# Weight split ring of a two-block model on one core: five slots for four, both engines four pieces ahead for three, six raw slots for five

## The reference

```python
def first_block(x, p, ...):
    for i in range(2):                                   # "layer a"
        h = mixer_block(h, ...)     # rmsnorm, h @ w_in, retention and gated delta rule, w_br_*, w_out
        u = rmsnorm(h, norm_ffn[i])
        h = h + (swiglu(u, ...) if i == 0 else moe(u, ...))   # 8 experts, top 2
        h = h + sigmoid(rmsnorm(h, norm_ple[i]) @ w_ple_gate[i]) * (p[i] @ w_ple[i])
    return rmsnorm(h, norm_final)
def second_block(x, ...):
    for l in range(2):                                   # "layer b": mLSTM, attention, HGRN2, squared-relu MLP
        ...
def gated_delta_rule(q, k, v, g, beta):                  # chunks of 64: a unit lower triangular solve per chunk
    u = triangular_solve(eye + a_mat, v * beta); w = triangular_solve(eye + a_mat, ...)
```

## Time and profile before

| | us |
| --- | --- |
| timed runs: 2141.18, 2141.46, 2144.6; median | 2141.46 |
| span of the profiled execution | 2140.0 |
| PE busy | 2083.7 (97%) |
| DVE busy | 1531.2 (72%) |
| ACT busy | 1361.4 (64%) |
| POOL busy | 65.4 (3%) |

### The profile page before, as it was taken

One profiled execution on the slowest core, in us unless ns is written; L12 is line 12 of the kernel. 1 busy time (PEld: TensorE's weight loads), 2 busy tenths in 40 slices (PEclk: granted clock), 3 DMA queues, 4 the chain that ended last, 5 costly groups with the idle time before them and its releaser, 6 DMA issues.

```text
span 2140.0 us, 37171 instructions
## 1 busy us (share of the span) xinstructions
PE 2083.7 (97%) x15388; PEld 1944.3 (91%) x15388; DVE 1531.2 (72%) x2200; ACT 1361.4 (64%) x1879; POOL 65.4 (3%) x102
## 2 busy tenths in 40 slices
PE   8999999999999989999999999999999999999999
PEld 7988999999989889998888888888889999979999
DVE  6777556766577675566999899977868665876664
ACT  5765575554567755657777777776766545776553
POOL 0013000000000130000000000000000000000000
PEclk9999999999999999999999999999999999999999
DMA  7424345565554343455999999954415565524554
GB/s 272 149 95 139 99 155 175 180 193 188 169 172 153 96 142 98 150 183 189 337 331 334 334 333 333 349 192 151 131 60 179 189 194 163 158 70 138 190 191 133
DMA packets 126448, 400.59 MB, mean 187 GB/s; under 512 B 26048, under 2 KB 26432, under 8 KB 126272
## 3 DMA queue, kind: packets, MB, share of 16 engines
q1 hardware_dynamic: 126272, 398.14, 56.0%
HBM read 395.72 MB, written 2.36 MB: 186 GB/s over the span
## 4 chain that ended last, share of the span: by engine, by line
PE 81%; ACT 8%; DVE 7%; issue 2%; POOL 2%; DMA 1%; SPq 0%; ACTq 0%; DVEq 0%; POOLq 0%
PE ps L493 80%; DVE wlo L2186 2%; ACT whi L1409 2%; ACT arena L1419 2%; ACT scr L1419 2%; DVE arena L2194 1%; ACT L1419 1%; DVE arena L2186 1%; POOL arena L3166 1%; ACT L1413 1%; DVE scr L2186 1%; POOL arena L3169 1%; DVE h L2186 1%; ACT rst L1419 1%; PE ps L1086 0%
## 5 line engine op out<-in xcount | busy, mean ns | idle before, releaser
L2186 DVE TENSOR_TENSOR wlo<-raw,whi 128x1024 fp32r<-128x1024 f32 (+2 forms) x622 | 745.5, 1212 | 283.7 <-ACT whi L1409 278.5
L1409 ACT ACTIVATE whi<-raw 128x1024 fp32r<-128x1024 f32 (+2 forms) x622 | 643.1, 1042 | 321.9 <-PE ps L493 315.2
L493 PE MATMUL ps<-uh,whi 128*128 128x256 f32 x2240 | 644.2, 288 | 10.9 <-DVE arena L2194 4.2
L493 PE MATMUL ps<-uh,wlo 128*128 128x256 f32 x2240 | 632.2, 282 | 0.0
L493 PE MATMUL ps<-ul,whi 128*128 128x256 f32 x2240 | 625.8, 279 | 0.0
L493 PE MATMUL ps<-arena_r,whi 128*128 128x256 f32 x2720 | 473.4, 279 | 2.9 <-DVE arena_r L2186 2.0
L493 PEld LDWEIGHTS ps<-uh,whi 128*128 128x128 f32 x2240 | 420.2, 188 | 23.9 <-issue 14.6
L493 PEld LDWEIGHTS ps<-ul,whi 128*128 128x128 f32 x2240 | 421.8, 188 | 4.2 <-issue 3.8
L493 PEld LDWEIGHTS ps<-uh,wlo 128*128 128x128 f32 x2240 | 419.4, 187 | 0.0
L493 PEld LDWEIGHTS ps<-arena_r,whi 128*128 128x128 f32 x2720 | 411.6, 188 | 5.8 <-DVE arena_r L2186 3.4
L493 PE MATMUL ps<-arena_r,wlo 128*128 128x256 f32 x1360 | 376.7, 277 | 0.0
(11 more groups left out here) (186 smaller groups left out, 2186.8 us busy)
## 6 DMA issues: line engine op xcount, KB each, us to landing
raw<-stream SPq DMA_DIRECT2D x586, 512.0 KB, 4.2
arena<-stream SPq DMA_DIRECT2D x64, 512.0 KB, 5.6
CO<-stream SPq DMA_DIRECT2D x44, 512.0 KB, 5.4
raw<-stream SPq DMA_DIRECT2D x32, 384.0 KB, 4.4
arena<-stream SPq DMA_DIRECT2D x20, 384.0 KB, 4.3
CO<-stream SPq DMA_DIRECT2D x12, 384.0 KB, 4.6
CO<-const SPq DMA_DIRECT2D x3, 683.0 KB, 6.9
h<-xT SPq DMA_DIRECT2D x4, 256.0 KB, 6.4
```

The lines of the kernel that those rows point to most:

```text
L493: return self.e.matmul(o, l, r, start=start, stop=stop, skip_group_check=True)
L1409: self.e.activation(M.whi[:, b:b + n], M.raw[a][:, 0:n], ACT.Copy).then_inc(K.sem("weight_hi"), 1)
L2186: return self.e.tensor_tensor(o, a, b, op)
```

## The change

Three constants are raised by one each, and the reservation of on-chip memory for the descriptors of transfers that GpSimd would issue is cut. No transfer of this kernel is issued by GpSimd. LATER is not changed.

```diff
-NRAW = 5
+NRAW = 6
 MORE = 5
-NSPLIT = 4
-AHEAD = 3
+NSPLIT = 5
+AHEAD = 4
...
-    nc = bacc.Bacc("TRN2", target_bir_lowering=False, num_devices=1)
+    nc = bacc.Bacc("TRN2", target_bir_lowering=False, num_devices=1,
+                   dynamic_dma_scratch_size=1024)
```

## The result

The changed kernel takes 2162.0 us (median of 4 runs, 2160.3 to 2163.4), the kernel before, measured beside it, 2141.3 us (4 runs, 2140.1 to 2144.6). The ratio is 1.0096, with a 95% interval of 1.0077 to 1.0115: 0.96% slower, 20.7 us by the medians. The prediction was 2162 us.

What follows compares the result with a forecast made beforehand. The prediction took PE to bound the kernel, busy 2083.7 of 2140.0 us. Holds 18.1 + clock 4.0 - gain 1.9 = 20.2 us gave a span of 2160.2 and a median of 2162 us, range 2153 to 2168 (8 in 10).

Steps and rivals of the forecast that it cites:

- What bounds the kernel: PE, busy 2083.7 of 2140.0 us and full in the experts; the change can give back at most 56 us.
- Place A: Pieces 43 and 216, sent behind the first block transfers in layers a, land late: GpSimd's chain 3.3 and 2.2 us late.
- the first rival: DVE catches up the 3.3 us before GpSimd's start at 171.97; the hold stays: 14.8 us, 2156 us; chance 0.17.
- Place B: Pieces 52 and 225, sent behind the stores of GpSimd's inverses, hold ACT; PE loses 9.4 and 8.7 us, 18.1 together.
- the second rival: Longer hold: waits at 198.30 and 788.98 stay, clock costs 2.6 us each time, gain used up: 26 us, 2168; chance 0.12.
- The clock: PE at half clock behind both new idle times in layers a: 2.0 us each, 4.0 together, between 2.4 and 5.2.
- The gain: Earlier splits remove PE's six short waits for low halves, at most 2.6 us; 1.9 us taken.
- the terms that I gave as nothing: Sixth raw slot, one more split ahead of the first layer's factors, cut reservation, order inside the experts: no cost.
- The sum: 18.1 + 4.0 - 1.9 = 20.2 us; the trace's span of 2140.0 us becomes 2160.2, the median 2162 us.
- The list of waits: Sign in the changed kernel's trace: ACT's waits for its transfers grow from 5.1 us to about 30.
- The third rival: Not slower: no hold, or PE's filler covers it; only a gain of 1.9 to 2.6 us, 2139 us; chance 0.09.
- Its deciding point: Landing of piece 52: leaving SP by 184.3 lets ACT copy by 188.7, with the pair at 189.74 on time.

Runs made afterwards that it cites:

- experiment 2: Changed kernel with only the two LATER limits ahead of the waits for GpSimd's inverses raised, 10 to 11: 2142.8 us, ratio 1.0013.
- experiment 1: Changed kernel with all nine entries of LATER raised by one: 2140.1 us, ratio 0.9995 to the kernel before.
- experiment 5: Changed kernel with NSPLIT back to 4 and AHEAD back to 3, keeping six raw slots and the cut reservation: 2141.4 us, ratio 0.9989.
- experiments 9: Changed kernel with AHEAD back to 3 and all entries of LATER raised by one, in more rounds: 2136.8 us, ratio 0.9979.
- 10: Changed kernel with NRAW back to 5, NSPLIT raised to 6 and all entries of LATER raised by one: 2134.8 us, ratio 0.9971.
- Experiments 7: Changed kernel with AHEAD back to 3 and all entries of LATER raised by one, first series: 2137.8 us, ratio 0.9979.

## Why the prediction was right

**What bounds the kernel.** PE does, and the experts are full in both kernels, as read. The gain that the change could bring was rightly bounded by small waits.

**Place A** (forecast: 3.3 us of lag in layer 0, 2.2 in layer 1, whole on GpSimd's chain). ACT's copy of piece 43 waited for its transfer, and GpSimd started at 174.02 in place of 171.97, 2.05 us later. But GpSimd had taken up the first chunk 1.1 us earlier than before (at 150.76 in place of 151.86), so against the work around it the lag is 3.15 us. In layer 1, from the first chunk to the second on GpSimd, it is 774.35 - 752.03 = 22.32 us where it was 763.56 - 743.47 = 20.09: 2.2 us, as forecast. So the lag was not caught up, as the first rival would have it. I had counted nothing for PE at place A itself, since it has filler there. That was not so in layer 0, where PE stood idle for 1.0 us at work that had no idle time before:

```profile
161.70 1.81 PE L493 MATMUL ps<-arena 128*128 128x128 f32 x12 [1.01 <-DVE arena L2186]
```

With no hold behind it, the lag of the inverses still shows, partly, in PE's wait for them at 197.34 (1.96 us in experiment 2, 1.21 before). In the changed kernel that does not stand beside the hold, since the hold covers it.

**Place B** (forecast: PE resumes 10.6 and 10.4 us late, less the absorbed waits of 1.21 and 1.71 us, 18.1 us). The mechanism came as written: the same call, the same instruction on PE, the same releaser. PE resumed 9.0 us late in layer 0. The forecast had 10.6, and the 1.6 us between them are two terms: piece 52 left at 194.41 and not at 195.6, since GpSimd and SP were 1.1 us earlier in this stretch than before, and it landed after 4.0 us and not 4.4. ACT's work behind it took 3.05 us where I had added up 3.1. The waits for the inverses at 198.30 and 788.98 are gone, as forecast, and with them the second rival. In layer 1 PE resumed at 801.40 in place of 782.66, 18.7 us later, 9.1 of which it brought from layer 0: 9.6 for the forecast's 10.4. The net by place is 9.1 us for layer 0 and 8.9 for layer 1, clock included; the forecast had 11.4 and 10.7, less the gain of 1.9. I had ACT's idle time as about 13 us, and it was 15.34 and 14.77. I had counted from 186.99; but before, too, ACT came to this call earlier, at 182.86, and stood there until 186.99 for the end of piece 47 on PE (the 4.13 us in rows 6, and 4.12 us in experiment 1). The changed kernel waits for the same end there, and the list puts the whole wait down to the transfer, which came last. This costs nothing, as the end of the hold is set by the transfer.

**The clock** (forecast 4.0 us, between 2.4 and 5.2). The two stretches lost 2.0 and 2.3 us, where I took 2.0 for each, at most 2.6 from the start of the program. (The clock column of rows 10 reads 1.00 there, but the matmuls of 512 columns start 0.43 us apart up to 15.3 us and 0.23 us apart behind, so the reading as half clock stands.) What I left out is that the stretch at 182.6 could go away: it gave 1.5 us back, and the change brought 2.8 us. That PE's busy time grew by 4.6 us is owed to the stretches at 1431 and 1557, which had no part in the forecast. The levels themselves are best read from single matmuls. PE in layer 0 of the changed kernel, at the low clock and then at the high one:

```profile
204.59 0.41 PE L493 MATMUL ps<-uh,whi 128*128 128x256 f32 x1
204.80 0.41 PE L493 MATMUL ps<-ul,whi 128*128 128x256 f32 x1
205.02 0.41 PE L493 MATMUL ps<-uh,wlo 128*128 128x256 f32 x1
...
205.82 0.28 PE L493 MATMUL ps<-uh,whi 128*128 128x256 f32 x1
205.93 0.28 PE L493 MATMUL ps<-ul,whi 128*128 128x256 f32 x1
```

From start to start it is 0.21 us at the low level and 0.11 to 0.12 us at the high one (the window at full clock has 3.20 / 27 = 0.119; the prediction's 0.114 is a little low). By the rule of the Trainium skill, TensorE: Matmul & The Clock Gate, "Wait — 56ns, not 53.3ns?", it would be, as an estimate for 256 columns, 213 and 109 ns: the trace agrees at the low level and lies some 10 ns above it at the high one.

**The gain** (forecast 1.9 us, at most 2.6). PE's waits for low halves fell by 1.4 us, by 1.6 with the limits raised. That kernel's median is 2.4 us under the kernel before, within what can be told from no change. Of the terms that I gave as nothing, the raw slots and the reservation were nothing (experiment 5).

**The sum.** 18.1 + 4.0 - 1.9 = 20.2 us was forecast for the span and 19.0 came. By terms it was 16.2 us of idle time where 14.4 came, and 4.0 us of clock where the change brought 2.8: both too high, by 1.8 and 1.2 us. The other 1.8 us of busy time, from stretches of the clock that belong to no term, made up for part of that. The mechanism, both places and the order of the terms were right; that the median is right to 0.1 us is luck. The list of waits was the weakest of the signs that I named: "about 30" us for ACT's transfers, and it was 42.0. The two holds are 30.1 us of it; six short waits in the layers a (pieces 43, 48 and 49, and 216, 221 and 222) add 8.6, and four at the start of the program 3.3.

**The third rival** (not slower). Its deciding point was that piece 52 leave SP by 184.3. It left at 194.41. Experiment 1 is this rival made true: with the limit raised, the piece goes ahead of the stores, and the time is that of the kernel before. The rule named beside it, to double-buffer (the Trainium skill, Trainium Kernel Development and Optimization, "Best Practices"), holds here for a slot that is free (experiments 9 and 10, 0.2 and 0.3%), not for one that comes with a lead that the queue doesn't follow.

## What to carry to other kernels

When a prefetch is made deeper, look at every queue that feeds it for places where its order is fixed by number: the consumer moves ahead, the producer doesn't, and the engine between them, which works strictly in order, stands before a transfer with ready work behind it. Price such a wait by what stands behind the waiting instruction and who waits for that; here 26 us of waiting cost 2.7 us by the medians and 30 us cost 13.6 (8.4 and 15.7 us of PE's idle time). Lead and number of slots are two knobs: a slot more than the lead needs halved the producer's waits for a release (353.5 to 177.5 us) and came with the gain of 0.2%, while raising both by one left them at 349.1 us (experiment 1) with no gain that can be told. That the gain comes through these waits is argued and not shown.

## What I had not expected of the hardware

**Half clock after a short idle time comes and goes.** Idle times of PE of 1.5 to 2 us near 180 us were followed by 3.3 us at 0.50 before and by full clock in the changed kernel. Around the long ones (11.75 and 10.84 us) it fell both times. The stretch at 1431 of the changed kernel is at 1410 in experiment 1, and the kernel before has full clock there. The row is of experiment 1, columns as in rows 3:

```profile
1410.00:1413.20 3.20, 3.20 (x16) 3.20 (x16) 2.40 (x5) 1.47 (x4) 0.00 (x0) 0.50 0.77 292
```

**The same kernel differs by some us in busy time.** Experiments 7 and 9 are one kernel. The pages of the two, the first and then the second:

```profile
span 2132.6 us, 37066 instructions
...
PE 2079.6 (98%) x15388; PEld 1941.1 (91%) x15388; DVE 1525.0 (72%) x2200; ACT 1347.4 (63%) x1879; POOL 65.4 (3%) x102
```
```profile
span 2136.1 us, 37066 instructions
...
PE 2086.4 (98%) x15388; PEld 1948.4 (91%) x15388; DVE 1525.6 (71%) x2200; ACT 1348.6 (63%) x1879; POOL 65.4 (3%) x102
```

PE is busy 6.8 us longer in the second with the same instructions, at a mean granted clock of 0.993 against 0.996. So a difference of under 7 us in PE's busy time between two single profiles, the 4.6 us of the result among them, can't be put down to a change by the total alone. Of these, the matmuls at the two places and at 182.6 carry 2.8 us. What decides in which execution the clock falls stays open.
